# Eight column pieces of two attention stages computed by products of 512 columns

## The reference

```python
# first block, differential attention: 512 columns of queries, 512 of keys
q, k, v = jnp.split(cols.astype(jnp.float32), 3, axis=-1)
q = q.reshape(bsz, seq, DIFF_HEADS, 2, DIFF_HEAD_DIM) * (DIFF_HEAD_DIM ** -0.5)
s = jnp.einsum('bqhcd,bkhcd->bhcqk', qb, kb)

# layer 0 of the second block, stick breaking attention: heads 0 to 7 (parts Q0 and K0)
z = jnp.einsum('bhqd,bhkd->bhqk', q_blk, k).astype(jnp.float32) * scale
log_keep = jnp.where(strict, jax.nn.log_sigmoid(-z), 0.0)
suffix = lax.cumsum(log_keep, axis=3, reverse=True)
weight = jnp.where(strict, jnp.exp(jax.nn.log_sigmoid(z) + between), 0.0)
```

## Time and profile before

| | |
|---|---|
| median of 3 executions | 1415.09 us (1414.96 to 1415.43) |
| the profiled execution | 1415.34 us, of which the span of the trace is 1413.4 us |
| TensorE, matmul | 1406.8 us busy (100%), 9197 matmuls |
| TensorE, weight loads | 1197.1 us (85%) |
| VectorE | 1179.5 us (83%) |
| ScalarE | 819.2 us (58%) |
| granted TensorE clock | 1.00 over the whole span |

### The profile page before, as it was taken

One profiled execution on the slowest core, in us unless ns is written; L12 is line 12 of the kernel. 1 busy time (PEld: TensorE's weight loads), 2 busy tenths in 40 slices (PEclk: granted clock), 3 DMA queues, 4 the chain that ended last, 5 costly groups with the idle time before them and its releaser, 6 DMA issues.

```text
span 1413.4 us, 22918 instructions
## 1 busy us (share of the span) xinstructions
PE 1406.8 (100%) x9197; PEld 1197.1 (85%) x9197; DVE 1179.5 (83%) x1641; ACT 819.2 (58%) x1103; POOL 26.5 (2%) x93
## 2 busy tenths in 40 slices
PE   9999999999999999999999999999999999999999
PEld 8988778888888888889878888888888887888887
DVE  6876786898877898998868988988889798688897
ACT  7735474565447555555766665555555557665562
POOL 0000000000001100000000000000000000000000
PEclk9999999999999999999999999999999999999999
DMA  8441236555554555455434555545555453355543
GB/s 335 155 151 62 101 110 208 173 185 203 194 221 179 185 203 185 173 208 192 141 118 172 185 195 187 213 169 197 200 179 197 165 177 148 112 201 195 180 177 119
DMA packets 36105, 249.12 MB, mean 176 GB/s; under 512 B 4128, under 2 KB 4256, under 8 KB 6688
## 3 DMA queue, kind: packets, MB, share of 16 engines
q1 hardware_dynamic: 35712, 247.46, 49.4%
q10 hardware_dynamic: 288, 0.19, 0.1%
HBM read 246.59 MB, written 1.05 MB: 175 GB/s over the span
## 4 chain that ended last, share of the span: by engine, by line
PE 97%; DMA 1%; ACT 1%; DVE 0%; issue 0%; SPq 0%; DVEq 0%; ACTq 0%
PE ps L2219 24%; PE ps L2131 16%; PE ps L2133 15%; PE ps L2132 15%; PE ps L2226 13%; PE ps L2393 2%; PE ps L2203 1%; PE ps L2207 1%; PE ps L2209 1%; DMA raw<-ws 1%; PE ps L2307 1%; PE ps L2606 1%; PE ps L2586 1%; PE ps L2595 1%; PE ps L2378 0%; ACT hi L2649 0%
## 5 line engine op out<-in xcount | busy, mean ns | idle before, releaser
L3017 DVE TENSOR_TENSOR lo<-raw,hi 128x2048 fp32r<-128x2048 f32 (+1 forms) x230 | 525.0, 2283 | 60.3 <-ACT hi L2649 57.6
L2649 ACT CAST hi<-raw 128x2048 fp32r<-128x2048 f32 (+1 forms) x230 | 439.8, 1913 | 186.6 <-PE ps L2133 118.9
L2219 PE MATMUL ps<-h,hi 128*128 128x512 f32 x1504 | 359.0, 390 | 0.0
L2219 PEld LDWEIGHTS ps<-h,hi 128*128 128x128 f32 x1504 | 276.4, 188 | 52.5
L2131 PE MATMUL ps<-hi,a 128*128 128x512 f32 x516 | 205.0, 397 | 0.0
L2133 PE MATMUL ps<-hi,a 128*128 128x512 f32 x516 | 201.4, 390 | 0.0
L2132 PE MATMUL ps<-lo,a 128*128 128x512 f32 x516 | 201.2, 390 | 0.0
L2226 PEld LDWEIGHTS ps<-h,lo 128*128 128x128 f32 x1504 | 192.2, 190 | 7.9
L2226 PE MATMUL ps<-h,lo 128*128 128x256 f32 x1504 | 194.4, 282 | 0.0
L2846 ACT COPY a<-ps 128x256 f32<-128x256 f32 x208 | 76.1, 373 | 143.5 <-PE ps L2219 78.5
L2131 PEld LDWEIGHTS ps<-hi,a 128*128 128x128 f32 x516 | 96.9, 188 | 22.6 <-issue 2.4
(11 more groups left out here) (383 smaller groups left out, 1800.1 us busy)
## 6 DMA issues: line engine op xcount, KB each, us to landing
raw<-ws SPq DMA_DIRECT2D x229, 1024.0 KB, 4.8
X<-xin SPq DMA_DIRECT2D x8, 256.0 KB, 5.3
raw<-ws SPq DMA_DIRECT2D x2, 512.0 KB, 6.5
out<-X SPq DMA_DIRECT2D x4, 256.0 KB, 2.2
small<-small SPq DMA_DIRECT2D x1, 992.5 KB, 12.8
const<-const SPq DMA_DIRECT2D x1, 900.0 KB, 6.8
a<-row SPq DMA_DIRECT2D x1, 512.0 KB, 6.2
const<-const SPq DMA_DIRECT2D x1, 388.0 KB, 13.2
```

Of the source, the lines that this page charges most:

```text
L2219: t = e.matmul(b2(s["slots"][u]), wh[:, k, 128 * u:128 * u + 128], h2[:, k, :, :], start=k == 0, stop=last)
L2649: e.copy(hi[j % NSPL][:, n], raw[j % NRAW][:, n]).then_inc(hi_ready, 1)
L3017: e.tensor_tensor(lo[j % NSPL][:, n], raw[j % NRAW][:, n], hi[j % NSPL][:, n].bitcast(F), ALU.subtract).then_inc(lo_ready, 1)
```

## The change

The eight pieces of queries and keys (7 to 10 and 101 to 104) go by `wide_runs` in place of `cols_piece`. ScalarE copies the HL halves of the two banks straight to their place in `qT`, `kTt`, `Q` or `KK` (kind "halves", two copies of 256 columns). VectorE adds the HH halves to that place (`meet_halves`, two additions of 256 columns, each of which frees a bank), waits for its own two additions, and multiplies by 1/rms there in SBUF (one instruction of 512 columns). The reads are no longer emitted by the filler at the end of a piece: two new tracks, `queries` and `turns_out`, do it in turn with the other tracks. A new semaphore `scaled_v` tells when they are done: the first scores of the differential attention wait for the last `dqk`, and each `sb_z` for its `qk_a`.

```diff
+        def queries():
+            for n in range(4):
+                while len(to_scale) <= n:
+                    yield None
+                c, sl, other, at = to_scale[n]
+                yield "act", at
+                emit("halves", act=0.7, slots=(other, sl), qk="dq" if n < 2 else "dk", n=2 * n % 4, v=[half_a.add() for _ in range(2)])
+                halves = script[-1]["v"]
+                yield "dve"
+                emit("dqk", dve=1.4, slots=(other, sl), halves=halves, n=(c - 1792) // 128, v=scaled_v.add())
+                for x in (other, sl):
+                    give(x)
...
-            def dq(sl, c, nxt):
-                emit("dqk", dve=0.7, slot=sl, n=(c - 1792) // 128)
-                if nxt:
-                    emit_lo(nxt)
-                state["dk"] = sl
+            def dq(sl, c, nxt, other):
+                to_scale.append((c, sl, other, cur[0]))
+                emit_lo(nxt)
+                return True
...
-                yield from cols_piece("w_in", 0, c, "h", nm.h_needs, dq)
+                yield from wide_runs("w_in", 0, c, nm.h_needs, begin, dq)
...
+            def turns_out():
+                for i in range(4):
+                    while len(to_turn) <= i:
+                        yield None
+                    n, qk_, scale, at, slots, due_ = to_turn[i]
+                    yield "act", due_
+                    halves = emit("halves", act=0.7, slots=slots, qk=qk_, n=n, v=[half_a.add() for _ in range(2)])["v"]
+                    yield "dve"
+                    emit("qk_a", dve=1.4, slots=slots, halves=halves, qk=qk_, n=n, scale=scale, v=scaled_v.add())
+                    for x in slots:
+                        give(x)
+                    at[n] = at[n + 1] = (scaled_v.sem, scaled_v.n)
                     known[qk_, n] = known[qk_, n + 1] = cur[0]
...
-                            yield from cols_piece(wn, 0, c, "h", nm.h_needs, turned(part[0], c0, scale, at))
+                            yield from wide_runs(wn, 0, c, nm.h_needs, begin, turned(part[0], c0, scale, at))
...
-            tracks = [finish(), norms(0, count), norms(1, count)]
+            tracks = [finish(), norms(0, count), norms(1, count)] + [turns_out()] * (layer == 0)
...
-                        read_out(state["dk"])
+                        e.wait_ge(scaled_v.sem, state["dk"])
...
+                elif kind == "halves":
+                    to = halves_of(s)
+                    for u, x in enumerate(s["slots"]):
+                        ready(x)
+                        e.copy(to[:, u, :], b2(x)[:, 1, :]).then_inc(half_a.sem, 1)
...
+            def meet_halves(s, to):
+                for u, x in enumerate(s["slots"]):
+                    e.wait_ge(half_a.sem, s["halves"][u])
+                    e.tensor_tensor(to[:, u, :], b2(x)[:, 0, :], to[:, u, :], ALU.add).then_inc(free[x.b], 1)
+                for x in s["slots"]:
+                    read_out(x)
+                return to
...
-                    dst = (Q if s["qk"] == "Q" else KK)[:, s["n"]:s["n"] + 2, :]
-                    ready(sl)
-                    e.scalar_tensor_tensor(dst, b2(sl), s["scale"], RB2, ALU.mult, ALU.mult).then_inc(free[sl.b], 1)
+                    t = meet_halves(s, halves_of(s))
+                    e.scalar_tensor_tensor(t, t, s["scale"], RB2, ALU.mult, ALU.mult).then_inc(scaled_v.sem, 1)
```

More of the change, by code:

```diff
@@ L257, in program @@
         diag_ready = Sig(sem("diag_ready"))
+        scaled_v = Sig(sem("queries_scaled"))
         c_part = Sig(sem("c_part"))
@@ L1605, in diff @@
         def diff():
-            while "vd" not in state or "bonus" not in state:
+            while "vd" not in state or "bonus" not in state or "dk" not in state:
                 yield None
@@ L1663, in diff @@
             state["ob"] = pv
+        to_scale = []
+        def queries():
[10 more added lines that the diff above has]
+                    give(x)
+            state["dk"] = scaled_v.n
         to_shift = []
@@ L1697, in mixers_fill, with begin @@
                     yield from cols_piece("w_in", 0, c, "h", nm.h_needs, shift)
-            def dq(sl, c, nxt):
-                emit("dqk", dve=0.7, slot=sl, n=(c - 1792) // 128)
-                if nxt:
-                    emit_lo(nxt)
-                state["dk"] = sl
+            def dq(sl, c, nxt, other):
+                to_scale.append((c, sl, other, cur[0]))
+                emit_lo(nxt)
+                return True
+            def begin(sl, c, u):
+                pass
             for c in range(1792, 2816, 256):
-                yield from cols_piece("w_in", 0, c, "h", nm.h_needs, dq)
+                yield from wide_runs("w_in", 0, c, nm.h_needs, begin, dq)
             def vd(sl, b, h):
@@ L1744, in mixers_fill @@
                                     pb(half))
-        weave([shifts(), rwkv_decays(), rwkv_keys(), (rwkv_chain(), LEAD), (rwkv_block(0), LEAD), (rwkv_block(1), LEAD),
+        weave([shifts(), queries(), rwkv_decays(), rwkv_keys(), (rwkv_chain(), LEAD), (rwkv_block(0), LEAD), (rwkv_block(1), LEAD),
                (rwkv_out(0), LEAD), (rwkv_out(1), LEAD), (diff(), LEAD + 2.0), gates()],
@@ L1974, in vv, with evac, begin @@
                 return evac
+            to_turn = []
             def turned(qk_, c0, scale, at):
-                def evac(sl, c, nxt):
-                    n = (c - c0) // 128
-                    emit("qk_a", dve=0.65, slot=sl, qk=qk_, n=n, scale=scale)
-                    at[n] = at[n + 1] = (free[sl.b], sl.n)
+                def evac(sl, c, nxt, other):
+                    to_turn.append(((c - c0) // 128, qk_, scale, at, (other, sl), cur[0]))
+                    emit_lo(nxt)
+                    return True
+                return evac
+            def turns_out():
[10 more added lines that the diff above has]
+                    at[n] = at[n + 1] = (scaled_v.sem, scaled_v.n)
                     known[qk_, n] = known[qk_, n + 1] = cur[0]
-                    if nxt:
-                        emit_lo(nxt)
-                return evac
+            def begin(sl, c, u):
+                pass
             rope = [("gq", "gqs", gqt, gqst), ("gk", "gks", gkt, gkst)] if layer == 0 else \
@@ L2608, in tensor_program, with halves_of @@
                     t.then_inc(full[sl.b], 1)
+        def halves_of(s):
+            return {"Q": Q, "K": KK, "dq": qT, "dk": kTt}[s["qk"]][:, s["n"]:s["n"] + 2, :]
         def scalar_program(e):
@@ L3356, in vector_program @@
                     n = s["n"]
-                    ready(sl)
-                    if n < 4:
-                        e.scalar_tensor_tensor(qT[:, n:n + 2, :], b2(sl), 0.125, RB2, ALU.mult,
-                                               ALU.mult).then_inc(free[sl.b], 1)
-                    else:
-                        e.tensor_tensor(kTt[:, n - 4:n - 2, :], b2(sl), RB2, ALU.mult).then_inc(free[sl.b], 1)
+                    t = meet_halves(s, halves_of({"qk": "dq" if n < 4 else "dk", "n": n % 4}))
+                    t = e.scalar_tensor_tensor(t, t, 0.125 if n < 4 else 1.0, RB2, ALU.mult, ALU.mult)
+                    t.then_inc(scaled_v.sem, 1)
                 elif kind == "gate_in":
```

## The result

| | before | after |
|---|---|---|
| median of 5 executions | 1415.18 us (1414.96 to 1415.51) | 1422.69 us (1421.24 to 1424.39) |
| ratio, 95% interval | | 1.0054 (1.0043 to 1.0065) |
| the profiled execution: time, span | 1415.34, 1413.4 us | 1421.24, 1419.4 us |

The changed kernel is slower by 7.5 us; 1419.6 had been forecast, with 1415.0 to 1423.0 as the range. One thing stands out before any trace is opened: its executions lie 3.2 us apart, those of before 0.6.

What follows compares the result with a forecast made beforehand. TensorE, without idle time, was taken to bound the kernel. Stage one's -0.4 and stage two's +4.9 us sum to +4.5 on 1415.34, giving 1419.8; the median lies 0.25 lower, 1419.6 us, range 1415.0 to 1423.0.

Steps and rivals of the forecast that it cites:

- What bounds the kernel: Both stages: TensorE has no idle time; each microsecond off its products is won, each wait lost unless replacing another.
- What the products save: Pieces 7 to 10 and 101 to 104: 5.55 us in place of 5.76 each, 1.66 us saved in all.
- rival D: Changed pieces: products of 512 columns run no cheaper than two of 256; +6.2 us, 1421.3 us; chance 0.04.
- The smaller saving by the Trainium skill's figures: Changed pieces: by 262 and 518 cycles a piece goes from 5.24 to 5.20 us, all eight saving 0.3 us.
- Stage two: Pieces 101 to 104 and what follows: 0.83 us saved, waits of 0.3, 3.3 and 2.1 us; sum +4.9 us.
- The 2.1 us in front of `sb_sum`: Stage two: TensorE arrives at `sb_sum` of pair 0 at 682.5 and waits for `sb_low`, ready at 684.6.
- the 3.3 us at `sb_z`: Stage two: TensorE reaches `sb_z` of pair 2 at 670.7 and waits for K0's last read, over at 673.9.
- Rival A: Stage two's waits don't come, the last read being over at 670.7; 1.66 us saved, 1413.5 us; chance 0.15.
- Rival B: Stage two: waits at `sb_z` and `sb_sum` are one lag counted twice; +1.7 us, 1416.9; chance 0.18 including times up to the forecast.
- Rival C: Lag goes on: a DMA lands in 6.5 us, not 4.9, delaying `hi` 107; +8.6 us, 1423.7; chance 0.12.
- Stage one: Pieces 7 to 10 and what follows: 0.83 us saved, waits 0.75, fewer trips give back 0.3; sum -0.4 us.
- For these waits the bounds are 0 and 2.1 us: Stage one: waits at the third `score` and `v_turn` bounded, all half as long again; stage between -1.1 and +1.3 us.

Runs made afterwards that it cites:

- stage2_only: Kernel before with only pieces 101 to 104 (stage two) by products of 512 columns: 1419.84 us, +4.7 against before, ratio 1.0034.
- lo107_behind_read: As `stage2_only`, but VectorE makes `lo` of piece 107 behind the last read of K0, not ahead: 1419.86 us, +4.8 against before.
- stage1_only: Kernel before with only pieces 7 to 10 (stage one) by products of 512 columns: 1417.79 us, +2.7 against before, ratio 1.0017.
- stage1_padded: As `stage1_only`, plus 128 idle waits of TensorE in pieces 7 to 10: -0.4 us against before, ratio 0.9997.
- reads_first: As `stage2_only`, but the track reading the four pieces goes first in ties (lead of 2 us): 1417.86 us, +2.8 against before, ratio 1.0020.

## Why the prediction was right, and where it was not

- **What bounds the kernel:** right. The loss is pauses of TensorE and a slow clock behind one of them. That its busy time is the same within 0.2 us doesn't show this: the 1.66 us saved and the longer records at the lower clock both stand in it.
- **What the products save:** right. In TensorE's timeline after, piece 7 (its starts 56.38, 60.03 and 61.95) takes 3.65 us for the products by `hi` and 1.92 for those by `lo`, as in the earlier trace rows; rival D has fallen:

```profile
56.38 3.82 PE L2255 MATMUL ps<-h,hi 128*128 128x512 f32 x16
60.03 2.08 PE L2262 MATMUL ps<-h,lo 128*128 128x256 f32 x16
61.95 0.40 PE L2255 MATMUL ps<-h,hi 128*128 128x512 f32 x1
```

  The smaller saving by the Trainium skill's figures ("TensorE: Matmul & The Clock Gate", section "Back-to-back issue gap") isn't what this stream has. The section gives them for single products, without a budget for the weight load, and here each product has one: the trace decides, at 0.228 us for 512 columns.
- **Stage two:** +4.9 forecast, +4.7 measured. The sum of VectorE's work held: in `stage2_only` TensorE comes to `sb_z` of pair 2 at 671.1 (forecast 670.7) and starts it at 674.44 (forecast 674.0); the first `sb_sum` starts at 684.83 (forecast 684.6). Two terms were put down to the wrong thing. The 2.1 us in front of `sb_sum` are 0.2; most of the rest was lost before it, to the clock: seven products of 512 columns took 3.10 us in place of 1.59 in the whole change, and in `stage2_only` the 16 products of `sb_z` 2.86 in place of 1.5. The time at `sb_sum` is set by ScalarE's chain, and TensorE may be late or wait, it is the same. And the 3.3 us at `sb_z` are not the last read's alone, as `lo107_behind_read` shows.
- **Rival A,** that the end turns on when the last read is over, names the wrong point as far as it was tested: 1.9 of the 3.2 us that it asked for were won back on VectorE, and the time didn't move. **Rival B,** one lag counted twice, was right in its idea (one chain of ScalarE is behind both waits) and wrong in its price: my walk had followed that chain to its end, so the sum already held it once. Its +1.7 doesn't follow from its condition either: without the 2.1 us the sum gives +2.4, without the 3.3 it gives +1.2. **Rival C** did not happen: nothing is lost behind the first `sb_sum` but 0.25 us at 707.
- **Stage one:** -0.4 forecast, +2.7 measured; this is the step that failed, and it is nearly all of the 3 us between forecast and result. "For these waits the bounds are 0 and 2.1 us" took the known waits alone (and speaks of three where the text names two; half as long again would be 1.1). Their sizes were, if anything, too high: the third `score` starts 0.58 us behind the last product ahead of it and `v_turn` 0.48, where such a trip takes 0.34, so 0.24 and 0.14 were lost and not 0.5 and 0.25. What was missing is a cost that no row of before has: the pauses in which TensorE has no instructions, 0.65 and 0.84 us in the trace of the whole change and 2.7 + 0.4 = 3.1 us between the medians of `stage1_only` and the forecast. Only what the change took out of the list could have hinted at it. With the pauses nearly gone (`stage1_padded`, -0.4) the stage comes out as forecast, though that run can't be told from no change.
- **The range** held the result, by 0.3 us, because C reached to 1423, not because of C's mechanism. That was luck: 3 us of the 7.5 come from something that the prediction doesn't name.

## What to carry to other kernels

Where TensorE has no idle time, a form that saves 4% of a piece but can't be interrupted is worth less than the order it breaks: count what is queued ahead of each read, follow the chain through all engines, and test whether a second wait stands behind the first before paying to remove it. A change in the number of instructions can cost time far behind itself, in the densest run of small products; put the count back with idle waits before judging the change. Wide scatter of executions was the first sign of it, and counting instructions to the pause is the quickest test: here all stood at the same place in a portion.

## What the runs showed of the hardware

- TensorE's instructions arrive in portions of 16 KB, 256 of them. In runs of 64x64 products (128 instructions in 1.09 us) TensorE stood for up to 1.2 us without a releaser, always between two portions, until 1.3 to 1.6 us behind the end of the next one's transfer (nine pauses in six traces). The loss had the portion's period: +2.7 and +3.2 us at 128 instructions less and more, 0.0 at 256 more, -0.4 and +1.0 us at 64 less and more.
- 512 idle waits of TensorE (256 instructions) between products of 256 columns cost nothing that shows (1415.30 against 1415.27 us).
- Behind 3.1 us without a product the granted clock was 0.50 for some 3.4 us and products of 512 columns took 0.43 us each. It also fell behind waits of 1.2 and 1.6 us with eight small products between them, and came back while TensorE worked at the lower level. In `reads_first`, whose longest wait was 1.1 us, it didn't fall.
